# First block of a two-block network: later retention heads, one square for eight exponentials, six modulation blocks read in two passes

## What is computed

```python
xn = rms_norm(x, norm_in_g)
q, k, v, g_ret, x_lru, g_lru = split(xn @ w_in)            # 1024 x 6144
o_ret = group_norm_heads(chunkwise_retention(rotary(q), rotary(k), v))   # 8 heads
y_ret = o_ret * silu(g_ret)
xc    = causal_depthwise_conv(x_lru)
r, i  = sigmoid(block_diag(xc, gate_a)), sigmoid(block_diag(xc, gate_x))
log_a = -8 * r * softplus(-lru_lambda)
a     = exp(log_a)
mult  = sqrt(max(1 - exp(2 * log_a), 0))                   # exp(2 log_a) = a * a
h_t   = a_t * h_(t-1) + mult * (i * xc)                    # a scan over the tokens
y_lru = h * silu(g_lru)
out   = rms_norm(x + concat(y_ret, y_lru) @ w_out, norm_out_g)
```

## Time and profile before

| | |
|---|---|
| median of 3 runs | 1706.65 us |
| the profiled execution, whole | 1706.55 us |
| its span, first to last instruction | 1704.8 us |
| PE busy | 1670.0 us, 98% |
| DVE busy | 1256.5 us, 74% |
| ACT busy | 842.9 us, 49% |
| mean granted TensorE clock | 0.998 |

### The profile page before, as it was taken

The page is one execution under the profiler, slowest core; times in us unless marked ns, Lnnn a source line. Parts: engine busy times, 40 slices in busy tenths (PEclk is TensorE's granted clock), DMA queues, the critical chain, the costliest instruction groups (busy, mean ns, idle before and its releaser), DMA issues.

```text
span 1704.8 us, 25221 instructions
## 1 busy us (share of the span) xinstructions
PE 1670.0 (98%) x9808; PEld 1426.1 (84%) x9808; DVE 1256.5 (74%) x2205; ACT 842.9 (49%) x1370; POOL 0.2 (0%) x4
## 2 busy tenths in 40 slices
PE   9989999999999999999999999999999999999998
PEld 9888888777787778888888888889778989979997
DVE  7999777875778798856877775347756786678874
ACT  6665555554324443347444442336553455466653
POOL 0000000000000000000000000000000000000000
PEclk9999999999999999999999999999999999999999
DMA  8646543232234335533545556324322444547653
GB/s 340 228 161 236 193 152 108 67 123 62 69 111 161 121 133 186 206 128 99 141 149 188 191 196 222 99 75 139 101 83 64 134 147 152 172 156 169 196 198 124
DMA packets 79078, 254.91 MB, mean 150 GB/s; under 512 B 14320, under 2 KB 18672, under 8 KB 78320
## 3 DMA queue, kind: packets, MB, share of 16 engines
q1 hardware_dynamic: 73488, 244.91, 43.8%
q10 hardware_dynamic: 5472, 8.39, 1.5%
HBM read 252.19 MB, written 1.07 MB: 149 GB/s over the span
## 4 chain that ended last, share of the span: by engine, by line
PE 78%; DVE 13%; ACT 5%; issue 3%; DMA 0%; ACTq 0%; DVEq 0%
PE bank L725 66%; DVE w_lo L1830 3%; PE bank L868 2%; PE bank L1037 2%; PE bank L1023 2%; PE bank L1115 2%; PE bank L1014 2%; ACT w_hi L1225 1%; DVE mod_w L1887 1%; PE bank L1104 1%; DVE probT L1887 1%; DVE att L2460 1%; DVE xc L1930 1%; DVE resid_x L2326 0%; DVE bank L2458 0%
## 5 line engine op out<-in xcount | busy, mean ns | idle before, releaser
L1830 DVE TENSOR_TENSOR w_lo<-w_raw,w_hi 128x1024 fp32r<-128x1024 f32 (+1 forms) x356 | 426.9, 1210 | 253.5 <-ACT w_hi L1225 251.9
L1225 ACT ACTIVATE w_hi<-w_raw 128x1024 fp32r<-128x1024 f32 (+1 forms) x356 | 370.0, 1048 | 339.2 <-PE bank L725 284.5
L725 PE MATMUL bank<-hT_hi,w_hi 128*128 128x512 f32 (+1 forms) x1280 | 446.0, 348 | 1.7 <-ACT zo L1555 0.6
L725 PE MATMUL bank<-hT_hi,w_lo 128*128 128x512 f32 (+1 forms) x1280 | 437.5, 342 | 0.0
L725 PE MATMUL bank<-hT_lo,w_hi 128*128 128x512 f32 (+1 forms) x1280 | 437.3, 342 | 0.0
L725 PEld LDWEIGHTS bank<-hT_hi,w_hi 128*128 128x128 f32 x1280 | 242.2, 189 | 30.4 <-issue 3.1
L725 PEld LDWEIGHTS bank<-hT_hi,w_lo 128*128 128x128 f32 x1280 | 242.1, 189 | 27.9
L725 PEld LDWEIGHTS bank<-hT_lo,w_hi 128*128 128x128 f32 x1280 | 242.4, 189 | 27.1 <-issue 1.0
L1887 DVE SCALAR_TENSOR_TENSOR mod_w<-mod_w,c_rows 128x1024 f32<-128x1024 f32 x96 | 117.0, 1218 | 8.4 <-DMA mod_w<-in_mod_weights 8.4
L725 PE MATMUL bank<-w_hi,hT_hi 128*128 128x512 f32 x272 | 114.7, 422 | 0.4 <-issue 0.4
L725 PE MATMUL bank<-w_lo,hT_hi 128*128 128x512 f32 x272 | 106.6, 392 | 0.0
(11 more groups left out here) (393 smaller groups left out, 2794.9 us busy)
## 6 DMA issues: line engine op xcount, KB each, us to landing
w_raw<-in_weights SPq DMA_DIRECT2D x356, 512.0 KB, 3.9
mod_w<-in_mod_weights SPq DMA_DIRECT2D x96, 512.0 KB, 4.1
nbias<-in_window_bias ACTq DMA_DIRECT2D x32, 128.0 KB, 3.2
resid_c<-in_ctx ACTq DMA_DIRECT2D x2, 1024.0 KB, 6.8
...
```

What stands on the lines that cost most here:

```text
L725: mm = pe.matmul(held[key][:, oc], st, mv_, start=(opens and k == 0 and t == 0 and i == 0), stop=(closes and k == tiles - 1 and t == 2), s ...
L1225: a.activation(w_hi[:, p % RING, :, used], w_raw[:, p % RING, :].rearrange("p (k n) -> p k n", k=KP)[:, :, used], ACT.Copy).then_inc(hi_re ...
L1830: v.tensor_tensor(w_lo[:, p % RING, :, used], w_raw[:, p % RING, :].rearrange("p (k n) -> p k n", k=KP)[:, :, used], w_hi[:, p % RING, :, ...
```

## The change

1. **Skip of eight steps.** `retention_early` starts with `EARLY_SKIP` 8 in place of 0: a step is a (piece, bank) pair, so the six steps follow pieces 25, 27, 29, 31, 33 and 35.
2. **One square.** The eight exponentials of 2 log_a fall away. ACT computes a = exp(log_a) in place (eight instructions), then one `Square` over all 128 x 2048 numbers, then the root. The clamp on DVE waits for the one square.
3. **Modulation in jobs.** The list of jobs replaces the list of blocks. Jobs 0 to 9 are blocks 0 to 9 with two passes, jobs 10 to 15 are blocks 10 to 15 with the context pass alone, jobs 16 to 21 load these six blocks again for the image pass, behind pieces 48, 48, 50, 50, 56 and 57. All that counts used blocks is raised by six.
4. **Order on DVE and ACT.** `mult * (i * xc)` is made in two halves, the modulation calls move, each scan waits for the instruction before it, and the splits are placed anew.

```diff
-MOD_SLOTS, EARLY_MODS, EARLY_SLOTS = 2, 16, 4
+MOD_SLOTS, EARLY_SLOTS = 2, 4
+FIRST_MODS, APART = 16, 6
+EARLY_MODS = FIRST_MODS + APART
...
     at = [5, 6, 7, 9, 12, 15, 18, 21, 24, 27, 30, 34, 37, 40, 42, 44]
+    at += [48, 48, 50, 50, 56, 57]
...
+def mod_jobs():
+    apart = range(FIRST_MODS - APART, FIRST_MODS)
+    jobs = [(m, (1,) if m in apart else (0, 1)) for m in range(FIRST_MODS)]
+    jobs += [(m, (0,)) for m in apart]
+    jobs += [(m, (0, 1) if m < MOD_BLOCKS + BOTH_MODS else (0,)) for m in range(FIRST_MODS, LAYERS * MOD_BLOCKS)]
+    return jobs
...
-                    sp.dma_start(mod_slot[slot], mods_in[m]).then_inc(mod_loaded[slot], 16)
+                    sp.dma_start(mod_slot[slot], mods_in[jobs[m][0]]).then_inc(mod_loaded[slot], 16)
...
-            early = Beside(retention_early(), RET_EVERY, 0)
+            early = Beside(retention_early(), RET_EVERY, EARLY_SKIP)
...
+            act.wait_ge(*A.last())
             for n in range(HEADS):
-                act.wait_ge(*lru_ix.at(n))
-                a.activation(xc[:, n, :], lru_r[:, n, :], ACT.Exp, scale=lam[:, 1, n:n + 1]).then_inc(*A.tell(lru_e2, n))
+                a.activation(lru_r[:, n, :], lru_r[:, n, :], ACT.Exp, scale=lam[:, 0, n:n + 1]).then_inc(*A.tell(lru_a, n))
                 if n % 4 == 3:
                     split_hi(23 + n // 4)
             act.wait_ge(*A.last())
+            act.wait_ge(*lru_ix.at(HEADS - 1))
+            a.activation(xc[:], lru_r[:], ACT.Square).then_inc(*A.tell(lru_e2, 0))
             tok(4, v1, ACT.Copy)
-            for n in range(HEADS):
-                a.activation(lru_r[:, n, :], lru_r[:, n, :], ACT.Exp, scale=lam[:, 0, n:n + 1]).then_inc(*A.tell(lru_a, n))
-                if n % 4 == 3:
-                    split_hi(25 + n // 4)
+            split_hi(26)
...
             def lru_scan(n):
+                dve.wait_ge(*W.last())
                 dve.wait_ge(*lru_a.at(n))
...
-            for n in range(4, HEADS):
+            for n in range(4, HEADS - 1):
                 lru_input(n)
             mod_ops(2)
+            lru_input(HEADS - 1)
             split_lo(23)
             mod_ops(2)
-            dve.wait_ge(*lru_e2.at(HEADS - 1))
+            dve.wait_ge(*lru_e2.at(0))
```

More of the change, by code:

```diff
@@ L659, in _ @@
                 load_at[piece("w_down", l, 0) + 5] = l, "ffn"
-            after = mod_after()
+            after, jobs = mod_after(), mod_jobs()
             m = 0
@@ L1874, in modulations @@
             def modulations():
-                for m in range(LAYERS * MOD_BLOCKS):
+                for i, (m, sets) in enumerate(mod_jobs()):
                     l, j = divmod(m, MOD_BLOCKS)
-                    sets = 2 if l == 0 or j < BOTH_MODS else 1
-                    split_lo(after[m] - 1)
-                    slot, count, _ = mod_place(m)
+                    split_lo(after[i] - 1)
+                    slot, count, _ = mod_place(i)
                     dve.wait_ge(mod_loaded[slot], 16 * count)
-                    if m:
-                        dve.wait_ge(mod_used, m)
-                    for s in range(sets):
+                    if i:
+                        dve.wait_ge(mod_used, i)
+                    for s in sets:
                         w = mod_slot[slot]
-                        product = w if s == sets - 1 else junk_of_mod(m)
+                        product = w if s == sets[-1] else junk_of_mod(m)
                         mm = v.scalar_tensor_tensor(product, w, 1.0, c_rows[:, s, :], ALU.mult, ALU.mult,
                                                     accum_out=modT[:, l, j, s:s + 1])
-                        mm.then_inc(*(W.next() if s < sets - 1 else (mod_used, 1)))
+                        mm.then_inc(*((mod_used, 1) if s == sets[-1] else W.next()))
                         yield
@@ L1933, in conv_pair, with ret_decay @@
                     W.mark(conv_ready, n)
-            def ret_decay(h):
+            def ret_decay(h, more=0):
                 key = ("rs", h)
-                ahead(key)
+                ahead(key, more)
                 dve.wait_ge(*filled_at(key))
@@ L2056, in _ @@
             split_lo(25)
-            mod_ops(2)
+            mod_ops(1)
             split_lo(26)
-            dve.wait_ge(decay_loaded, 16)
-            ret_decay(0)
-            dve.wait_ge(*lru_mult.at(0))
-            v.tensor_tensor(lru_i[:], lru_i[:], xc[:], ALU.mult).then_inc(*W.next())
-            dve.wait_ge(*W.last())
-            ret_decay(1)
-            ret_norm(0)
-            for n in range(3):
-                lru_scan(n)
+            dve.wait_ge(*lru_mult.at(0))
+            lru_drive(0)
@@ L2068, in _ @@
+            split_lo(27)
+            lru_drive(4)
+            split_lo(28)
+            dve.wait_ge(decay_loaded, 16)
+            ret_decay(0, -2)
+            for n in range(4):
+                lru_scan(n)
+            split_lo(29)
+            ret_decay(1, -2)
+            ret_var_of(0, -2)
+            split_lo(30)
+            ret_normed(0)
             for g in range(2):
-                ahead((("in", 5), g))
                 dve.wait_ge(*drained_at((("in", 5), g)))
             ret_gate(0)
-            ret_decay(2)
@@ L2073, in _ @@
-            lru_scan(3)
-            ret_norm(1)
+            for n in (4, 5):
+                lru_scan(n)
+            split_lo(31)
+            ret_decay(2, -2)
+            ret_var_of(1, -2)
+            lru_scan(6)
+            ret_normed(1)
             ret_gate(1)
+            split_lo(32)
             ret_lo(0)
-            lru_scan(4)
-            ret_decay(3)
-            lru_scan(5)
-            ret_norm(2)
+            lru_scan(7)
+            dve.wait_ge(*W.last())
+            for n in range(4):
+                lru_gating(n)
@@ L2081, in _ @@
+            ret_decay(3, -2)
+            split_lo(34)
+            ret_var_of(2, -2)
+            ret_normed(2)
             ret_gate(2)
             ret_lo(1)
-            for n in (6, 7):
-                lru_scan(n)
-            dve.wait_ge(*W.last())
-            split_lo(32)
+            for n in range(4, HEADS):
+                lru_gating(n)
+            split_lo(35)
+            ret_var_of(3, -2)
             for n in range(4):
-                lru_gating(n)
-            ret_norm(3)
+                lru_lo(n)
@@ L2101, in _ @@
             mod_ops(2)
+            ret_lo(3)
             split_lo(37)
```

75 lines of the change are left out of this document (40 added, 35 removed).

## The result

The changed kernel takes 1715.06 us (median of 5 runs, 1713.4 to 1715.66) against 1706.65; the ratio is 1.0047, 95% interval 1.0036 to 1.0058: 8.4 us slower. The profiled execution took 1715.63 us, 1713.8 of them its span. The forecast was 1713.2 in a range of 1705 to 1717.

What follows compares the result with a forecast made beforehand. DVE's list up to piece 44 was taken as the bound, PE waiting for it: -0.8 (to piece 37) + 5.8 (hold) + 2.6 (job 9, low part) - 0.9 = +6.7 us, forecast 1713.2, range 1705.0 to 1717.0.

Steps and rivals of the forecast that it cites:

- the hold: SP waits at job 12 until job 8 is used, pieces 38 to 40 queued behind; DVE idles 5.8 us before `w_lo` 38.
- `w_lo` 37: DVE begins it at 137.3, 0.8 us earlier than before.
- `w_lo` 39: After the hold, job 9 and a low part, PE begins piece 39 7.6 us later.
- piece 44: DVE's list from piece 39 holds the same work, so 7.6 us stays; PE begins it at 168 to 171.
- end of the span: Two passes fewer ahead of `w_lo` 46 give back 0.9 us behind piece 44, leaving +6.7 us.
- the clock follows: Slower rival: PE's clock halves after the wait ahead of piece 23, transfer perhaps 6.5 us; 1716.0 us, chance 0.13.
- The square's wait: DVE waits 4.6 us at the clamp for ACT's square (1.9 us); PE waits 2.7 us ahead of piece 23.
- Up to piece 37: DVE from `w_lo` 25: 42.5 us work plus 3.6 idle along the steps; -0.8 net of the square's wait.
- The transfer: Load of piece 38 behind job 12, taken at 5.4 us, inside the 5.8 us hold.
- Job 9 between `w_lo` 38 and 39: Job 9 and a low part now lie there on DVE's list: +2.6 us.
- From `w_lo` 39 to piece 44: DVE's list holds the same work as before, so no further change there.
- The deferral: Six deferred passes take only two passes, 2.3 us, out of the DVE-bound stretch; passes behind piece 44 cost nothing.

Runs made afterwards that it cites:

- E1: Changed kernel with jobs 12, 13 and 14 loaded behind pieces 40, 41 and 43 instead of 37, 40 and 42: 1708.78 us.
- E2: Changed kernel with `w_lo` 23 made ahead of the clamp instead of behind it: 1711.85 us.
- E4: Kernel before with the deferral of the image passes alone; retention, exponentials and splits as before: 1702.84 us.
- E9: E7 with three context passes moved behind piece 44 and loads of jobs 17 to 19 moved to behind pieces 49, 52, 53: 1703.19 us.
- E7: Changed kernel with `w_lo` 23 ahead of the clamp, jobs 7 to 9 moved up, nothing between `w_lo` 37 and 38: 1704.55 us.
- E3: Changed kernel with both edits, jobs 12 to 14 loaded later and `w_lo` 23 ahead of the clamp: 1706.90 us.

## Why the prediction was right, step by step

**The direction and the mechanism.** The time is 1.9 us above the forecast. The forecast of +6.7 rested on the hold of SP, and the hold is there (139.19 for job 12, "about 137" was said) and worth 6.3 us (E1). The rest of the steps, along the time at which DVE begins a `w_lo`, against before:

| point | forecast | profile |
|---|---|---|
| `w_lo` 37 | -0.8 | +1.0 (139.09; 138.09) |
| the hold | +5.8 | +5.11 |
| `w_lo` 39 | +7.6 | +8.8 (153.27; 144.46) |
| piece 44 | +7.6 | +9.4 (171.82; 162.43) |
| end of the span | +6.7 | +9.0 (1713.8; 1704.8) |

Against the forecast the steps are off by +1.8, -0.7, 0.0, +0.6 and, behind piece 44, +0.5 (I gave back 0.9 there, the profile has 0.4). So the smaller hold hid part of what I had left out. Piece 44 was to begin at 168 to 171 and began at 171.82. The measured 1715.06 is nearer to the 1716.0 of the rival "the clock follows" than to my 1713.2: the hold, which both have, is right, and that the forecast missed by no more than 1.9 is in part luck.

**The square's wait** was forecast at 4.6 us and PE's ahead of piece 23 at 2.7; the rows have 4.59 and 2.64. The square itself took 1.90 us, as taken from the root.

**Up to piece 37: mis-sized by 1.8 us.** I let the wait ahead of piece 23 cost nothing because DVE was the bound. The rival "the clock follows" named what happened: the clock halved behind it, at a chance of 0.13 that was too low. Through it the scores came late, and DVE's waits along the steps were 1.89, 1.70 and smaller ones, 4.4 in all from 92 to 138 us (4.1 for scores, 0.3 for a root), for the 3.6 counted. That is 0.8 of the 1.8. Some 0.4 is only this execution, late from its first `w_lo` on. DVE's work from `w_lo` 25 to `w_lo` 37 was 42.9 us and not 42.5, another 0.4; the rest is small. E2, which takes the stall away, leaves 2.4 us of idle time along the steps. So the stall costs 2.0 us there, and my 3.6 was too high for the case that I had in mind, a stall without a price, by 1.2: two errors that cancelled in part.

**The transfer** was taken at 5.4 us and took 4.7; the hold is smaller by that. (By the Trainium skill, DMA: Bandwidth & Descriptors, "where the ~2 µs actually goes" with the fit above it, which the page gives for DMAs issued from GpSimd, a transfer of 512 KB takes an estimated 3.2. Neither the first of the three nor the later ones, 5.5 and 6.3, agree; SP issued each of them within 0.5 us of another transfer.)

**Job 9 between `w_lo` 38 and 39** was +2.6; from `w_lo` 38 to `w_lo` 39 it is now 153.27 - 145.41 = 7.86 us, before 144.46 - (138.09 + 1.14) = 5.23, so +2.6.

**From `w_lo` 39 to piece 44: +0.6 that I had at nothing.** I wrote that DVE's list holds the same work. It does, but in another form: two passes of one job became two passes of two jobs, and the second waits for the first to be counted. DVE's timeline after, two passes and `w_lo` 40:

```profile
154.41 1.22 DVE L1904 SCALAR_TENSOR_TENSOR mod_w<-mod_w,c_rows 128x1024 f32<-128x1024 f32 x1
...
155.74 1.23 DVE L1904 SCALAR_TENSOR_TENSOR mod_w<-mod_w,c_rows 128x1024 f32<-128x1024 f32 x1
...
156.89 1.22 DVE L1848 TENSOR_TENSOR w_lo<-w_raw,w_hi 128x1024 fp32r<-128x1024 f32 x1
```

From pass to pass 1.33 us, from pass to `w_lo` 1.15: 0.18 for the wait, three times up to piece 44.

**The deferral** was costed by the passes that stand in the stretch, two fewer, so 2.3 us. That holds for this change, where other jobs filled the freed places. By itself it is worth 4.05 us (E4). For E4 I had bounded it by PE's idle time in the windows, 1.9 + 0.5, and that bound was too low, since busy time hides part of each wait.

**The whole loss, in one chain of runs.** From E4 at 1702.84 (medians; the kernel before had 1706.65 to 1707.00 in these sets, but the times of one kernel spread over 0.7 us (E7) to 2.6 us (E1), those of the changed kernel over 2.3: the first step is not clear of zero): late retention and the square, repaired, +0.35 (E9); three passes ahead of piece 44, and the loads as they were, +1.36 (E7); jobs 7 to 9 at the places of the change, with E1's load table, +2.35 (E3); `w_lo` 23 behind the clamp, +1.88 (E1); the hold, +6.28: 1715.06. The size of a step depends on where it stands in the chain: the first repair of `w_lo` 23 alone gave 3.2, behind E1 it gives 1.9.
